# Reordering the first layer's routing stage in a two-layer decoder step on one NeuronCore

## The reference, cut to what matters

```python
sh1, sc1, gt1, sh2, sc2, gt2 = silu(c) @ w_ada[i] + b_ada[i]        # conditioning, 6 x D columns
x = x + gt1 * mixer(rms_norm(x, norm_mix[i]) * (1 + sc1) + sh1)
h = rms_norm(x, norm_ffn[i]) * (1 + sc2) + sh2
s = sigmoid(h @ w_router);  sel = s + router_bias                   # 64 experts in 8 groups
keep 4 groups by the sum of their two best, then the 8 best experts of a token;  w = s / sum(s) * 2.5
y = sum over the 8 experts of w * (silu(h @ Wg[e]) * (h @ Wu[e])) @ Wd[e]
    + (silu(h @ Sg) * (h @ Su)) @ Sd                                # the shared expert, for all tokens
x = x + gt2 * y
```

## Time and profile before

| | |
|---|---|
| median of 3 runs | 1662.87 us |
| the profiled execution's own time | 1665.58 us |
| its span | 1663.6 us |
| TensorE matmul busy | 1588.1 us, 95% |
| VectorE, ScalarE, GpSimd busy | 706.3, 441.0, 147.8 us |
| mean granted TensorE clock | 0.988 of full |
| DMA traffic | 552.32 MB, mean 332 GB/s |
| layer 0's routing stage | about 228 to 285 us of the span |
| layer 0's experts | about 285 to 832 us |

### The profile page before, as it was taken

The page is one execution under the profiler, slowest core; times in us unless marked ns, Lnnn a source line. Parts: engine busy times, 40 slices in busy tenths (PEclk is TensorE's granted clock), DMA queues, the critical chain, the costliest instruction groups (busy, mean ns, idle before and its releaser), DMA issues. The chain is left out here.

```text
span 1663.6 us, 30044 instructions
## 1 busy us (share of the span) xinstructions
PE 1588.1 (95%) x11366; PEld 923.2 (55%) x11366; DVE 706.3 (42%) x1911; ACT 441.0 (27%) x980; POOL 147.8 (9%) x208
## 2 busy tenths in 40 slices
PE   5999998999999999999899988989999999999997
PEld 2667665555555555555467757755555555455554
DVE  3124553743433423324347863467433433433424
ACT  1211120222222222222232143312222222222223
POOL 0001300000000000000020052010000000000000
PEclk9999899999999999999999989999999999999999
DMA  9795657999999999999495246269999999999990
GB/s 367 296 349 185 241 226 312 369 391 414 417 415 416 416 411 414 415 416 410 171 324 187 99 153 202 103 250 385 400 417 416 416 415 414 415 415 416 413 365 27
DMA packets 131861, 552.32 MB, mean 332 GB/s; under 512 B 19408, under 2 KB 36638, under 8 KB 93399
## 3 DMA queue, kind: packets, MB, share of 16 engines
q1 hardware_dynamic: 113394, 513.82, 77.5%
q0 software_dynamic: 15392, 34.66, 5.9%
q10 hardware_dynamic: 3012, 3.00, 0.6%
HBM read 562.74 MB, written 8.60 MB: 343 GB/s over the span
## 5 line engine op out<-in xcount | busy, mean ns | idle before, releaser
L1435 PE MATMUL PS<-ring,arena 128*64 128x256 f32 x4288 | 490.6, 382 | 2.5 <-ACT arena L1761 1.5
L1435 PEld LDWEIGHTS PS<-ring,arena 128*64 128x64 f32 x4288 | 303.8, 137 | 182.9 <-issue 41.2
L1459 PE MATMUL PS<-ring,arena 128*64 128x512 f32 x1072 | 259.6, 605 | 1.4 <-ACT arena L1746 1.4
L1398 PE MATMUL PS<-arena 128*128 128x512 bf16 (+1 forms) x796 | 197.4, 384 | 0.0
L1664 DVE TENSOR_TENSOR arena<-arena,PS 128x128 f32<-128x128 f32 x134 | 38.6, 288 | 371.1 <-ACT arena L1744 365.1
L1648 DVE TENSOR_SCALAR arena<-arena 128x512 bf16<-128x512 f32 x130 | 62.8, 483 | 256.5 <-ACT arena L1755 256.5
L1754 ACT COPY arena<-PS 64x512 f32<-64x512 f32 x134 | 77.5, 578 | 302.2 <-PE PS L1459 302.2
L1459 PEld LDWEIGHTS PS<-ring,arena 128*64 128x64 f32 x1072 | 65.0, 136 | 120.4 <-issue 104.1
L1744 ACT ACTIVATE arena<-PS 128x128 f32<-128x128 f32 x134 | 37.2, 278 | 326.3 <-PE PS L1435 326.3
L1398 PEld LDWEIGHTS PS<-arena 128*128 128x128 bf16 (+1 forms) x796 | 69.6, 99 | 91.9 <-issue 27.7
L1389 PEld LDWEIGHTS PS<-cst,arena 128*128 128x128 f32 x552 | 72.1, 195 | 80.2 <-issue 78.3
(11 more groups left out here) (505 smaller groups left out, 1496.4 us busy)
## 6 DMA issues: line engine op xcount, KB each, us to landing
ring<-in_moe_w_gate SPq DMA_DIRECT2D x134, 1024.0 KB, 8.6
ring<-in_moe_w_up SPq DMA_DIRECT2D x134, 1024.0 KB, 10.8
ring<-in_moe_w_down SPq DMA_DIRECT2D x134, 1024.0 KB, 15.4
ring<-in_w_ada SPq DMA_DIRECT2D x36, 1024.0 KB, 10.7
ring<-in_gla_w_in SPq DMA_DIRECT2D x8, 1152.0 KB, 16.7
ring<-in_w_ada SPq DMA_DIRECT2D x8, 1152.0 KB, 8.6
ring<-in_dsa_w_in SPq DMA_DIRECT2D x6, 1024.0 KB, 20.3
arena<-in_state_gla POOLq DMA_DIRECT2D x8, 512.0 KB, 7.6
```

Source lines behind the costliest of these rows:

```text
L1398: ins_ = pe.matmul(PS[:, c, :], oh[:, T * P:(T + 1) * P], y[:, 512 * j:512 * j + 512], start=False, stop=True, skip_group_check=True)
L1435: m = pe.matmul(PS[64 * half:64 * half + 64, 5, 0:256].rearrange("p (g n) -> p g n", g=2), rows[:, k, CAP * b:CAP * b + CAP], gu[:, :, k, ...
L1459: m = pe.matmul(PS[64 * j:64 * j + 64, 7, :], hTt[b][:, kk * CAP:(kk + 1) * CAP], ring[:, s, 2, kk * D + 512 * j:kk * D + 512 * j + 512], ...
```

## The change

In layer 0:

- the 7 matmuls on constants ahead of the router are gone, and the sum of conditioning item 0 stands in their place;
- item 1's sum follows the turned token rows directly;
- both shared gate tiles run whole ahead of the wait for the mask, as in layer 1;
- behind the mask stand the first up tile, the first list group, item 2, the second up tile and item 3; the wait for the first list (bank 3 read) moves to just before unit 3's turn;
- unit 4 is turned in bank 4 (was bank 0), and the wait for `mod_T` 5 moves behind the 8 wide down matmuls of the shared expert (banks 0 to 3).

In both layers: the second norm's sum is in bank 1 (was 0), the router's logits are in bank 7 from column 192 (were in bank 0), the bank that is cleared for the lists (L1320) and the shared expert's sample rows (L1327) come after all 8 wide down matmuls, and no longer between them. In layer 1, the late fold is in bank 0 (was 7).

```diff
         def pe_norm_tile(n, k):
-            m = pe.matmul(PS[:, 0, 0:TOK], K["ones1024"], norm_sq[:, k, :], ...)
+            m = pe.matmul(PS[:, 1, 0:TOK], K["ones1024"], norm_sq[:, k, :], ...)
...
             if l:
                 pe_late_rows(7, 5)
             else:
-                pe_warm(7)
+                item_ready(pe, it_ada[1][0])
+                pe_ada_sum(1, 0, NEXT_SUM)
             pe.wait_ge(S("route_w"), PER["route_w"] * l + 32)
             for k in range(KT):
                 pe_chunk(2 * l + 1, k)
-                m = pe.matmul(PS[0:NE, 0, 0:TOK], wr[:, k, :], hT[:, k, 0:TOK], ...)
+                m = pe.matmul(PS[0:NE, 7, 192:192 + TOK], wr[:, k, :], hT[:, k, 0:TOK], ...)
...
             if l:
-                pe_late_fold(7, 7, 256)
+                pe_late_fold(7, 0, 256)
...
             if l == 0:
-                pe.wait_ge(S("hrow_sb"), 1)
-                item_ready(pe, it_ada[1][0])
-                pe_ada_sum(1, 0, NEXT_SUM)
+                item_ready(pe, it_ada[1][1])
+                pe_ada_sum(1, 1, NEXT_SUM)
             pe.wait_ge(S("hrow_sb"), PER["hrow_sb"] * l + 3)
             item_ready(pe, it_sh[l])
-            if l == 0:
-                shared_in(0, 0, range(4))
-                item_ready(pe, it_ada[1][1])
-                pe_ada_sum(1, 1, NEXT_SUM)
-            else:
-                shared_in(0, 0)
-                shared_in(0, 1)
+            shared_in(0, 0)
+            shared_in(0, 1)
...
             m.then_inc(S("route_pe"), 1)
+            shared_in(1, 0)
+            pe_lists(l, 0)
             if l == 0:
-                shared_in(0, 0, range(4, KT))
-                shared_in(0, 1, range(4))
-                pe_lists(0, 0)
-                shared_in(0, 1, range(4, KT))
-                pe.wait_ge(S("lists"), 1)
-                shared_in(1, 0)
                 route_dve(pe, 0, "nch")
                 item_ready(pe, it_ada[1][2])
                 pe_ada_sum(1, 2, NEXT_SUM)
-            else:
-                shared_in(1, 0)
-                pe_lists(l, 0)
             shared_in(1, 1).then_inc(S("route_pe"), 1)
             if l == 0:
                 item_ready(pe, it_ada[1][3])
                 pe_ada_sum(1, 3, NEXT_SUM)
+                pe.wait_ge(S("lists"), 1)
                 pe_ada_turn(3, 3)
...
             if l == 0:
-                pe_ada_turn(4, 0)
-                pe.wait_ge(S("mod_T"), 5)
-            pe.matmul(PS[:, 4, 256:466]..., K["ident"], hT[:, 0:2, TOK:TOK + 105], ...)
+                pe_ada_turn(4, 4)
             for kk in range(2):
                 for T in range(2):
                     for j in range(2):
                         pe.matmul(PS[:, 2 * T + j, :], hsS[:, kk, T * P:(T + 1) * P], wd2[:, kk, 512 * j:512 * j + 512], ...)
+            if l == 0:
+                pe.wait_ge(S("mod_T"), 5)
+            pe.matmul(PS[:, 4, 256:466]..., K["ident"], hT[:, 0:2, TOK:TOK + 105], ...)
+            for kk in range(2):
                 for j in range(4):
                     m = pe.matmul(PS[32 * j:32 * j + DEC, 4, 0:256], hsS[:, kk, SEQ:TOK], wd2[:, kk, 256 * j:256 * j + 256], ...)
...
# VectorE: dve_late(7, 7, 256) -> dve_late(7, 0, 256);  dve_ada_unit(4, 0) -> dve_ada_unit(4, 4)
# ScalarE: the exponential reads PS[0:NE, 7, 192:192 + TOK];  act_norm(1 and 3, norm_sq, 0) -> (..., 1)
```

More of the change, by code:

```diff
@@ L602, in pe_norm_tile @@
             pe.wait_ge(S("x_sq"), XSQ[n] + k + 1)
-            m = pe.matmul(PS[:, 0, 0:TOK], K["ones1024"], norm_sq[:, k, :], start=(k == 0), stop=(k == KT - 1), skip_group_check=True)
+            m = pe.matmul(PS[:, 1, 0:TOK], K["ones1024"], norm_sq[:, k, :], start=(k == 0), stop=(k == KT - 1), skip_group_check=True)
             if k == KT - 1:
@@ L1241, in pe_route @@
                 pe_chunk(2 * l + 1, k)
-                m = pe.matmul(PS[0:NE, 0, 0:TOK], wr[:, k, :], hT[:, k, 0:TOK], start=(k == 0), stop=(k == KT - 1))
+                m = pe.matmul(PS[0:NE, 7, 192:192 + TOK], wr[:, k, :], hT[:, k, 0:TOK], start=(k == 0), stop=(k == KT - 1))
             m.then_inc(S("route_pe"), 1)
@@ L1317, in pe_route @@
             if l == 0:
-                pe_ada_turn(4, 0)
-                pe.wait_ge(S("mod_T"), 5)
-            pe.matmul(PS[:, 4, 256:466].rearrange("p (a n) -> p a n", a=2), K["ident"], hT[:, 0:2, TOK:TOK + 105], start=True, stop=True, skip_group_check=True)
+                pe_ada_turn(4, 4)
             for kk in range(2):
@@ L1325, in pe_route @@
                                   start=(kk == 0), stop=(kk == 1), skip_group_check=True)
+            if l == 0:
+                pe.wait_ge(S("mod_T"), 5)
+            pe.matmul(PS[:, 4, 256:466].rearrange("p (a n) -> p a n", a=2), K["ident"], hT[:, 0:2, TOK:TOK + 105], start=True, stop=True, skip_group_check=True)
+            for kk in range(2):
                 for j in range(4):
@@ L1542, in dve_route @@
             if l:
-                dve_late(7, 7, 256)
+                dve_late(7, 0, 256)
             route_dve(dve, l, "e")
@@ L1601, in dve_route @@
             if l == 0:
-                dve_ada_unit(4, 0)
+                dve_ada_unit(4, 4)
             dve_sel(l, 1)
@@ L1723, in act_route @@
             route_pe(act, l, "logits")
-            act.activation(eT[0:NE, 0:TOK], PS[0:NE, 0, 0:TOK], ACT.Exp, scale=-1.0).then_inc(S("route_exp"), 1)
+            act.activation(eT[0:NE, 0:TOK], PS[0:NE, 7, 192:192 + TOK], ACT.Exp, scale=-1.0).then_inc(S("route_exp"), 1)
             for T in range(TT):
@@ L2627, in _ @@
             act_gla()
-            act_norm(1, norm_sq, 0)
+            act_norm(1, norm_sq, 1)
             act_shift(1, 0, 1)
@@ L2635, in _ @@
             act_dsa()
-            act_norm(3, norm_sq, 0)
+            act_norm(3, norm_sq, 1)
             act_shift(3, 1, 1)
```

## The result

The changed kernel took 1652.64 us (median of 5 runs, 1650.39 to 1653.7) against 1662.87 us (5 runs, 1661.95 to 1668.8). The ratio is 0.9919, 95% interval 0.9904 to 0.9934. It is faster, as forecast, but by 13.5 us (11 to 16) by the ratio, where 8.8 were forecast. That puts it at 1649.4 us, and the range given ended at 1650.5. The ten runs shown here are 10.2 us apart by their medians and 11.9 by their means, so part of the 13.5 lies in how the ratio is formed, which the record does not show. Two later comparisons of the same two kernels gave 0.9942 (0.9927 to 0.9957) and 0.9926 (0.9910 to 0.9941). Over all comparisons the mean is 1664.94 us for before (the 55 runs of the later comparisons; the clocks of the five of the first are not on record) and 1653.82 for the changed kernel (17 runs), 11.1 us apart.

The account below looks back on a forecast made before the run. TensorE, busy 95% of the span, was taken as the bound. Gains of 5.52 + 1.99 + 1.69 = 9.20, less 0.4, gave 8.8 us and 1654.1 us from the median 1662.87; range 1650.5 to 1658.5.

Parts of the forecast that it names:

- The order, 5.52 us: Layer 0's routing stage: item 0's sum in the norm's hole and gate tiles filling the mask wait save 5.52 us.
- The wait for `modT` and what followed it: Before layer 0's wide down matmuls: removing the wait saves 1.99 us, and the clock fall after it 1.69 us.
- The 0.4 us taken off for the new hole: Ahead of layer 0's router: a hole grown to 1.49 us may lower the clock; cost 0.4 us, bounds 0 and 1.66.
- The experts pass it on: Layer 0's experts: loads are on time by 3 to 4 us, TensorE sets the pace, so the shift is kept.
- I take the same difference from the median: Final step: the 8.8 us taken from the profiled execution is also taken from the median, 1662.87, giving 1654.1 us.
- place (d): Layer 0's first 8 wide down matmuls: clock falls to 0.50 after the `modT` wait, 5.29 us against 3.60; 1.69 us gained.
- VectorE as the bound: Rival: behind the mask, VectorE's splits and selections set unit 3 and what follows; gain only 5.5 us, 1657.4; chance 0.07.
- The clock taking back: Rival: clock falls again in layer 0's stage, before the router or first expert; gain 6.0 us, 1656.9; chance 0.12.
- its second form: Clock fall before layer 0's first expert, costing 1.54 us; with only one of two falls 1655.3 us.
- No effect: Rival: the first gather or a load sets the first expert anyway; 1662.9 us; chance 0.04.
- the slower weight stream: Rival: in the experts, new load and gather phases cost 4% of the rate; 9.3 us slower, 1672.2; chance 0.05.
- The rule cited: Short idle times between matmul groups can swing the clock, so the fall at the wide down matmuls need not vanish.

Follow-up runs that it names:

- e2: Kernel before with only the new order up to unit 3's turn; unit 4 in bank 0 and its wait ahead of the wide down matmuls again; ratio 0.9965.
- g2: Kernel before with only the changed banks for the norm's sum, the router's logits and the late fold; ratio 1.0008.
- e1: The changed kernel again, in a second comparison beside the kernel before; ratio 0.9942.
- g1: The changed kernel in a third comparison beside the kernel before; ratio 0.9926.
- e4: Changed kernel with the constants' matmuls back in the norm's hole and item 0's sum back behind the turned rows; ratio to before 0.9954.
- f1: Kernel before with matmuls on constants put into layer 0's waits for the mask and `mod_T` 5, no work saved; ratio 0.9996.
- e3: Kernel before with only unit 4 turned in bank 4, and the `mod_T` 5 wait and sample rows behind the wide down matmuls; ratio 0.9976.
- f3: Changed kernel with more moved: a third of item 1 into the norm's hole, up-tile steps earlier in both layers; ratio to before 0.9918.
- f2: Changed kernel with matmuls on constants in the waits left ahead of layer 1's router and both layers' first experts; ratio to before 0.9916.

## Why the prediction was right and where it failed

**The order, 5.52 us:** right. The trace has 5.44 and e2 alone 5.57. The hole, the filled wait and the unchanged start of the mask's matmuls (17.29 us after the router in both) came as worked out.

**The wait for `modT` and what followed it, 1.99 + 1.69 = 3.68 us:** right against the profiled execution, a little low. From unit 4's turn to the shared expert's end the traces have 12.89 before (285.20 - 272.31) and 8.61 after (271.10 - 262.49), so 4.28. The 0.6 on top is the order of the matmuls, which I had taken at 0 between -0.6 and +0.6. Together the 16 wide ones take 7.03 us and the 16 of the sample rows 1.05, where pairs of 3.6 to 3.7 and 0.62 stood before; TensorE also starts 0.25 us after the turn's start and not after its 0.41. In layer 1, where there is no wait, the order alone gives 0.32: from the last turned tile's start to the last sample row's end 8.80 before, 8.48 after. The 1.69 is partly luck: it is what the profiled execution of before lost at this wait, and g2's lost nothing there.

**The 0.4 us taken off for the new hole:** wrong. The hole was 1.39 us (forecast 1.49), and the router took 3.77 us in all three profiles of the changed kernel. Layer 1's longer hole of about 2.0 us had the router at 5.43 in seven of ten profiles (e1, g1, e2, e4, f1, g2), and at 3.75 in three (the first of the changed kernel, e3, f3).

**The experts pass it on:** right. Their pace is 7.87 us against 7.86, the latest landing 17.6 us in both.

**The step that failed** is the last one, "I take the same difference from the median". It took the change of one profiled execution for the change of the runs, with the clock counted only at place (d) and a spread of about 1 us for other falls. Even its range allowed no more than 9.2 + 3.2 = 12.4 us. What the runs showed: the stage gave 9.7 us as traced, and the first comparison 13.5. The mean clock of the changed kernel's five runs was 0.9902 there, against 0.9874 for before's 55 later runs, 0.0028 more. At 1.02 us for each 0.001 that is 2.9 us, and with the 9.4 at equal clock it makes 12.3, inside the interval of 11 to 16. The last 1.2 us stay open; the means of the ten runs are only 11.9 apart. The second and third comparisons have 0.0009 and 0.0016 more, so 10.3 and 11.0, against 9.7 and 12.3 measured.

Two things lie behind the 1 to 3 us. The clock of the stretches that no edit touches differs from execution to execution (228.49 to 235.71 us up to layer 0's router), so that a comparison of five runs has luck in it. And pooled over the study, the changed kernel's clock is higher by 0.0016, 1.7 us. I argued only that waits removed take falls with them. In five profiles of kernels with one of the old waits or fills in their place (before, e2, e3, f1, g2) each had a fall between the router and the end of the first expert, in three of the changed kernel none. That the change causes the whole 1.7 us is not shown: e4 and f3 have neither old wait and had a fall at the first expert (5.36 us).

One sum stays open. Without any fall the stretch is 53.73 us in g2 and 45.69 in the changed kernel, 8.04 apart, and with layer 1's 0.32 that is 8.4 us, against 9.4 (error 0.4) at equal clock. No run shows where that 1.0 us is.

**The rivals.** VectorE as the bound: excluded by e2 and e3, which add, and by f3. The clock taking back: in the three profiles of the changed kernel there is no fall in layer 0's stage or first expert, and the runs' clock went up and not down. But its second form, a fall at the first expert, worth 1.69 us (5.36 against 3.67), did come in e4 and f3, which lack the old waits too, so it is not excluded for other executions. No effect and the slower weight stream: not seen.

**The rule cited** from the Trainium skill ("TensorE: Matmul & The Clock Gate", the section on depth-cycling) had more in it than I gave it. By the traces of f1, g2, e4 and f3 the clock fell at the small gaps of 0.33, 0.68 and 0.77 us ahead of the first expert, with the two old waits there, filled or gone. In the three profiles of the changed kernel it did not, with the same small gaps.

## What to carry to other kernels

Work that waits for nothing new belongs into the holes of a chain that another engine sets, until each hole is nearly full. Here such local sums from one trace came true to 0.1 us in layer 0 (5.44 for 5.52, 1.77 for 1.8) and to 0.2 in layer 1 (2.2 for 2.4). In e4 the sum missed by 1 us, where the next step hung on another engine that had time in hand. A comparison of medians carries on top of that the clock of stretches that nobody changed, so read each run's granted clock beside its time and compare at equal clock before explaining a surplus. Whether filling waits with idle matmuls wins anything is open here: f1 could tell no gain, f2 was 3.8 us faster by its mean, and the same fills on top of f3 gave nothing. And do not read the effect of an edit from one profile's fall of the clock: f1's looked like the work of its fills until g2 showed the same without them.

## What the runs showed of the hardware

- One kernel's runs differ by several us with the mean granted clock: 1659.1 to 1668.7 us for the kernel before at 0.985 to 0.991. The slope is 1.02 us for each 0.001, and 0.001 of 1660 us is 1.66 us of full-speed time; why the slope is smaller is not shown.
- The same wait brings the clock down in one execution and not in the next. The mask's wait of 2.85 us kept 1.00 in the kernel before, and the same wait of 2.84 us was followed by 0.50 in e3. The wait of 2.0 us for `modT` was followed by 5.29 us for 8 wide matmuls in before and by 3.59 us in g2. The wait of 2.0 us ahead of layer 1's router was followed by 5.43 us at that router in seven profiles, and by 3.75 us in three.
- Gaps of 0.33, 0.68 and 0.77 us among short turns can be followed by a fall: the first expert took 5.36 us behind them in f1, g2, e4 and f3, and 3.67 us in before and the three profiles of the changed kernel. In e4 and f3 TensorE had no longer wait than these in the 10 us ahead.
- The order of independent matmuls counts: in layer 1, groups of one shape issued together were 0.3 us shorter than the same groups in turn (8.48 against 8.80 us).
